# Eight places for the experts' weights in place of six, loops over groups of four experts, norm rows and bias in other buffers

## What is computed

```
def expert_block(args):
    xblk, e = args
    hcat = xblk @ w_up[e] + b_up[e]                 # 1024 -> 2048
    x_glu = jnp.minimum(hcat[:, 0::2], SWIGLU_LIMIT)
    x_lin = jnp.clip(hcat[:, 1::2], -SWIGLU_LIMIT, SWIGLU_LIMIT)
    act = x_glu * jax.nn.sigmoid(SWIGLU_ALPHA * x_glu) * (x_lin + 1.0)
    return act @ w_down[e] + b_down[e]              # 1024 -> 1024
...
contrib = y_slots[dest] * gate_sorted[:, None]
out = jax.ops.segment_sum(contrib, tok_sorted, num_segments=N)
...
h = layer_norm(DEEPNORM_ALPHA * h + ffn, ln2_g[l], ln2_b[l])
```

## Time and profile before

| | us |
|---|---|
| median of three timed runs (1586.87 to 1589.27) | 1588.96 |
| profiled execution | 1591.26 |
| its span, first to last instruction | 1589.5 |
| PE busy in the span | 1450.5 (91%) |
| weight loads of PE | 831.1 (52%) |
| DVE busy | 568.9 (36%) |
| ACT busy | 445.1 (28%) |
| experts' up products, L1239, 2048 of them | 452.6 |
| experts' down products, L1276, 1024 of them | 226.8 |

### The profile page before, as it was taken

One profiled execution on the slowest core, in us unless ns is written; L12 is line 12 of the kernel. 1 busy time (PEld: TensorE's weight loads), 2 busy tenths in 40 slices (PEclk: granted clock), 3 DMA queues, 4 the chain that ended last, 5 costly groups with the idle time before them and its releaser, 6 DMA issues. The chain is left out here.

```text
span 1589.5 us, 19014 instructions
## 1 busy us (share of the span) xinstructions
PE 1450.5 (91%) x7555; PEld 831.1 (52%) x7555; DVE 568.9 (36%) x1003; ACT 445.1 (28%) x569; POOL 36.7 (2%) x79
## 2 busy tenths in 40 slices
PE   7999999999999898898898898898896998789999
PEld 7988797333333333333333333333333877778887
DVE  3885456211120210210210211211114355557765
ACT  4654443221121111211112112112113135434443
POOL 1000030000000000000000000000000102000000
PEclk9999999999999999999999999999999998889999
DMA  8598997799999999999999999999997440335550
GB/s 246 164 310 264 329 335 249 322 426 429 428 428 428 428 429 429 429 429 428 428 428 428 428 428 428 428 429 428 429 429 250 133 159 28 105 107 186 186 185 27
DMA packets 130683, 516.92 MB, mean 325 GB/s; under 512 B 11173, under 2 KB 99086, under 8 KB 106030
## 3 DMA queue, kind: packets, MB, share of 16 engines
q1 hardware_dynamic: 130302, 515.11, 81.8%
q10 hardware_dynamic: 336, 1.18, 0.2%
HBM read 515.22 MB, written 1.05 MB: 325 GB/s over the span
## 5 line engine op out<-in xcount | busy, mean ns | idle before, releaser
L1239 PE MATMUL ps<-ring,xg 128*64 128x512 f32 x2048 | 452.6, 594 | 23.2 <-DMA ring<-in_expert_w_up 21.9
L1239 PEld LDWEIGHTS ps<-ring,xg 128*64 128x64 f32 x2048 | 143.9, 137 | 326.6 <-issue 269.4
L1352 DVE TENSOR_TENSOR glu<-ps,bupT 128x512 f32<-128x512 f32 x32 | 22.1, 692 | 739.3 <-PE ps L1248 739.3
L1276 PE MATMUL ps<-ring,act 128*64 128x512 f32 x1024 | 226.8, 595 | 6.9 <-DVE act L1362 6.9
L1276 PEld LDWEIGHTS ps<-ring,act 128*64 128x64 f32 x1024 | 70.7, 137 | 150.0 <-issue 127.9
L78 ACT ACTIVATE hrow<-ps 128x1024 f32<-128x1024 f32 x32 | 32.8, 1024 | 411.9 <-PE ps L1239 411.9
L1910 PE MATMUL ps<-h_halves,w_hi 128*128 128x512 f32 x352 | 125.8, 401 | 5.5 <-issue 5.5
L2007 DVE TENSOR_TENSOR w_lo<-ring,w_hi 128x2048 fp32r<-128x2048 f32 x37 | 84.8, 2292 | 70.7 <-ACT w_hi L78 70.7
L78 ACT ACTIVATE y<-ps 64x512 f32<-64x512 f32 x64 | 37.9, 592 | 241.0 <-PE ps L1276 240.7
L1912 PE MATMUL ps<-h_halves,w_lo 128*128 128x256 f32 x352 | 99.9, 284 | 0.0
L78 ACT ACTIVATE w_hi<-ring 128x2048 fp32r<-128x2048 f32 x37 | 70.6, 1909 | 69.1 <-PE ps L1912 41.7
(11 more groups left out here) (396 smaller groups left out, 1867.1 us busy)
## 6 DMA issues: line engine op xcount, KB each, us to landing
ring<-in_expert_w_up SPq DMA_DIRECT2D x128, 2048.0 KB, 23.4
ring<-in_expert_w_down SPq DMA_DIRECT2D x64, 2048.0 KB, 20.0
ring<-in_w_in SPq DMA_DIRECT2D x30, 1024.0 KB, 8.3
ring<-in_w_ada SPq DMA_DIRECT2D x24, 1024.0 KB, 6.0
ring<-in_w_gu SPq DMA_DIRECT2D x22, 1024.0 KB, 5.1
ring<-in_w_down SPq DMA_DIRECT2D x11, 1024.0 KB, 4.9
ring<-in_w_out SPq DMA_DIRECT2D x8, 1024.0 KB, 8.2
ring<-in_w_branch_sb SPq DMA_DIRECT2D x2, 1024.0 KB, 7.2
```

Source lines behind the costliest of these rows:

```text
L1239: last = nc.tensor.matmul(up[a2 * CAP:(a2 + 1) * CAP, u, :], k.xg[:, q, h * CAP:(h + 1) * CAP], w[:, c:c + 512], start=(q == 0), stop=(q = ...
L1276: last = nc.tensor.matmul(down[a2 * CAP:(a2 + 1) * CAP, :], k.act[:, m % 4, m // 4, :], w[:, c:c + 512], start=(m == 0), stop=(m == KF - 1 ...
L1352: link(nc.vector.tensor_tensor(k.glu[:, :, :, :], g, b[:, 0].to_broadcast(wide), ALU.add))
```

## The change

- `PLACES` is 8. Chunk i of a group goes to place i modulo 8; places 0 to 5 are those in the ring, 6 and 7 are a new buffer `more` of 32 KB a partition. There are eight semaphores `expert_in`, one a place.
- The loops of SP and PE go by groups of four experts (24 chunks, three turns through the eight places). PE's body holds two pairs in place of one; its loop has eight turns in place of sixteen. SP's loop has seven turns and a rest in place of 31. The loops of ACT and DVE stay loops over pairs.
- SP sends chunks 6 and 7, the first two of expert 1, at the head of `experts` without a wait on PE, behind the norm rows. After that chunk i waits until chunk i - 8 has been used (before: i - 6).
- The last uses of the ring's slots come at other counts, and the waits of the eight late loads follow (`2 * PLACES` for `PER`).
- To make room: `g2` and `b2` lie in the halves of `xT`; `b_dn` lies in the first 32 partitions of `hrow`; `k.bm` gets a buffer of its own, allotted after the experts' buffers are given back.
- Semaphores merged: `lb_ready` and `lf_ready` into one, `ln_in` of `branches` and `late_in` into one, with the counts of the waits adapted.

```diff
+PLACES = 8
+GROUP = 4 * CHUNKS
...
-def chunk_slot(c):
-    return (EARLY + 2 * c) % SLOTS
-def expert_chunk(k, c):
-    return k.ring[:, chunk_slot(c):chunk_slot(c) + 2, :].rearrange("p s n -> p (s n)")
-def load_expert(k, sp, a, e, c):
+def expert_chunk(k, i):
+    i %= PLACES
+    if i >= PLACES - 2:
+        return k.more[:, i - (PLACES - 2), :]
+    at = (EARLY + 2 * i) % SLOTS
+    return k.ring[:, at:at + 2, :].rearrange("p s n -> p (s n)")
+def expert_arrived(k, pe, group, i):
+    pe.wait_ge(k.expert_in[i % PLACES], group * (16 * GROUP // PLACES) + 16 * (i // PLACES + 1))
+    return expert_chunk(k, i)
+def load_expert(k, sp, a, first, i):
+    e, c = first + i // CHUNKS, i % CHUNKS
...
-    sp.dma_start(expert_chunk(k, c), src).then_inc(k.expert_in[c], 16)
+    sp.dma_start(expert_chunk(k, i), src).then_inc(k.expert_in[i % PLACES], 16)
...
             for dst, src in k.late_loads:
-                sp.dma_start(dst, src).then_inc(k.late_in, 16)
+                sp.dma_start(dst, src).then_inc(k.ln_in, 16)
             extra = extra_rounds(sp)
-            def refill(e, done):
-                for c in range(CHUNKS):
-                    sp.wait_ge(used, done + 2 * c + 2)
-                    load_expert(k, sp, a, e, c)
-            with sp.Fori(0, E - 1) as e:
-                refill(e + 1, e * PER)
+            for i in range(CHUNKS, PLACES):
+                load_expert(k, sp, a, 0, i)
+            def refill(first, done, lo, hi):
+                for i in range(lo, hi):
+                    sp.wait_ge(used, done + 2 * (i - PLACES + 1))
+                    load_expert(k, sp, a, first, i)
+            def rounds(done):
+                with sp.Fori(0, E // 4 - 1) as g:
+                    refill(g * 4, g * (2 * GROUP) + done, PLACES, GROUP + PLACES)
+                refill(E - 4, done + (E - 4) * PER, PLACES, GROUP)
+            rounds(0)
...
-                sp.wait_ge(used, done + (E * PER + q + 1 - PER))
+                sp.wait_ge(used, done + (E * PER + q + 1 - 2 * PLACES))
...
-            with pe.Fori(0, extra + 1) as r, pe.Fori(0, pairs) as p:
-                n = r * pairs + p
+            def pair(group, two, n):
                 pe.wait_ge(xg_ready, n + 1)
                 for h in range(2):
+                    first = (2 * two + h) * CHUNKS
...
                         if q % 2 == 0:
-                            pe.wait_ge(k.expert_in[q // 2], n * 32 + arrivals(q // 2, h))
-                        w = expert_chunk(k, q // 2)[:, (q % 2) * 2048:(q % 2 + 1) * 2048]
+                            chunk = expert_arrived(k, pe, group, first + q // 2)
+                        w = chunk[:, (q % 2) * 2048:(q % 2 + 1) * 2048]
...
+            with pe.Fori(0, extra + 1) as r, pe.Fori(0, pairs // 2) as g:
+                for two in range(2):
+                    pair(r * (pairs // 2) + g, two, r * pairs + g * 2 + two)
...
-            dve.wait_ge(k.late_in, 16 * len(k.late_loads))
+            dve.wait_ge(k.ln_in, 32 + 16 * len(k.late_loads))
...
-        k.gB, k.bm = k.x, k.xT[:, :, :].rearrange("p (t h) n -> p t h n", t=TT)
+        k.gB = k.x
...
-            k.g2, k.b2 = ht("g2", [P, D]), ht("b2", [P, D])
+            k.g2, k.b2 = (k.xT[:, 4 * n:4 * n + 4, :].rearrange("p k t -> p (k t)") for n in range(2))
...
-                k.gateT, k.b_dn = md("gateT", [E, T]), md("b_dn", [E, D])
+                k.gateT, k.b_dn = md("gateT", [E, T]), k.hrow[0:E, :]
+                k.more = md("more", [P, 2, 2 * SLOT])
...
+            k.bm = ht("bias_flipped", [P, TT, NA, T])
```

More of the change, by code:

```diff
@@ L613, in later @@
                     act.wait_ge(f_ready, 1)
-                    nc.scalar.activation(k.sgq[:, :, :], k.fbuf[:, :, :], ACT.Ln).then_inc(lf_ready, 1)
+                    nc.scalar.activation(k.sgq[:, :, :], k.fbuf[:, :, :], ACT.Ln).then_inc(lb_lf_ready, 1)
                 if i in (6, 7, 10, 11):
@@ L630, in _ @@
                     nc.scalar.activation(k.cact[:, :], k.cols[:, ROWS["c"]:ROWS["c"] + KD], ACT.Sigmoid)
-                    nc.scalar.activation(lb, k.lb[:, 8:12], ACT.Sigmoid).then_inc(lb_ready, 1)
+                    nc.scalar.activation(lb, k.lb[:, 8:12], ACT.Sigmoid).then_inc(lb_lf_ready, 1)
                 if i == 7:
@@ L740, in _ @@
                 if i == 2:
-                    dve.wait_ge(lb_ready, 1)
+                    dve.wait_ge(lb_lf_ready, 1)
                     nc.vector.tensor_tensor(k.cact[:, :], k.cact[:, :], k.cols[:, ROWS["c"]:ROWS["c"] + KD], ALU.mult)
@@ L753, in _ @@
                 if i == 5:
-                    dve.wait_ge(lf_ready, 1)
+                    dve.wait_ge(lb_lf_ready, 2)
                     dve.wait_ge(f_ready, 1)
@@ L829, in branches @@
         "logits_done", "top_negmax", "top_exp", "chosen", "pos_done"))
-    ln_in, gd, gb_done, ang_ready = (sem(n) for n in ("ln1_in", "gate_diag", "gate_rows", "angles"))
+    gd, gb_done, ang_ready = (sem(n) for n in ("gate_diag", "gate_rows", "angles"))
     gates, m, hT, xs = k.gates, k.xT, k.hT1, (k.xhi, k.xlo)
@@ L1034, in _ @@
             dve.wait_ge(k.x_in, 64)
-            dve.wait_ge(ln_in, 32)
+            dve.wait_ge(k.ln_in, 32)
             link(nc.vector.memset(k.mv[:, :, :], 0.0))
@@ L1155, in _ @@
             for dst, src in k.late_loads:
-                sp.dma_start(dst, src).then_inc(k.late_in, 16)
+                sp.dma_start(dst, src).then_inc(k.ln_in, 16)
             extra = extra_rounds(sp)
-            def refill(e, done):
-                for c in range(CHUNKS):
-                    sp.wait_ge(used, done + 2 * c + 2)
-                    load_expert(k, sp, a, e, c)
-            with sp.Fori(0, E - 1) as e:
-                refill(e + 1, e * PER)
+            for i in range(CHUNKS, PLACES):
[9 more added lines that the diff above has]
+            rounds(0)
             with sp.If(extra > 0):
                 with sp.Fori(0, extra) as r:
-                    refill(0, r * (E * PER) + (E - 1) * PER)
-                    with sp.Fori(0, E - 1) as e:
-                        refill(e + 1, r * (E * PER) + e * PER + E * PER)
+                    refill(0, r * (E * PER) + E * PER, 0, PLACES)
+                    rounds(r * (E * PER) + E * PER)
             done = extra * (E * PER)
@@ L1202, in scatter @@
                     last.then_inc(sc_done, 1)
-            def arrivals(c, h):
-                return 16 * (h + 1)
             for t in range(TT):
@@ L1267, in _ @@
                     for j in range(4):
-                        c4 = UP_CHUNKS + j // 2
                         if j % 2 == 0:
-                            pe.wait_ge(k.expert_in[c4], n * 32 + arrivals(c4, h))
-                        w = expert_chunk(k, c4)[:, (j % 2) * 2048:(j % 2 + 1) * 2048]
+                            chunk = expert_arrived(k, pe, group, first + UP_CHUNKS + j // 2)
+                        w = chunk[:, (j % 2) * 2048:(j % 2 + 1) * 2048]
                         for kk in range(2):
@@ L2134, in program @@
         k.last_used = k.sem("last_used")
-        k.expert_in = [k.sem(f"expert_in{i}") for i in range(CHUNKS)]
+        k.expert_in = [k.sem(f"expert_in{i}") for i in range(PLACES)]
         k.expert_used = k.sem("expert_used")
-        k.bcast_in, k.late_in, k.bias_in, k.bm_in = (k.sem(n) for n in (
-            "bcast_in", "late_in", "bias_in", "bm_in"))
+        k.bcast_in, k.ln_in, k.bias_in, k.bm_in = (k.sem(n) for n in (
+            "bcast_in", "ln_in", "bias_in", "bm_in"))
         k.evac, k.ln_var, k.ln_root, k.turned, k.hT_ready, k.sums, k.roots = (k.sem(n) for n in (
```

6 lines of the change are left out of this document (3 added, 3 removed).

## The result

| | before | after |
|---|---|---|
| median of the timed runs, us | 1589.12 | 1578.61 (1578.09 to 1580.43) |
| ratio, 95% interval | 1 | 0.9939 (0.9926 to 0.9951) |
| span of the profiled execution, us | 1589.47 | 1578.60 |
| start of the loop (first up product of PE) | 281.78 | 282.45 |
| last copy of y, which ends the loop | 1210.08 | 1202.09 |

The kernel is 0.61% faster, 10.5 us by the medians (1589.12 is the median of before with a fourth run, of three it was 1588.96) and 10.9 us by the two spans. Those 10.87 us split into three parts: the loop is 8.66 shorter, it starts 0.67 later, and the tail is 2.88 shorter.

What follows compares the result with a forecast made beforehand. The prediction took DMA transfers to bound the experts' loop from 540 us to its end. A term of -9.79 us, all others 0, gave span 1579.7, less 2.3 to the median: 1579.2 us, range 1575.0 to 1585.0.

Steps and rivals of the forecast that it cites:

- The bound: Experts' loop: DMA transfers bind from 540 us to its end and hold that end back by 31.2 us.
- The term of -9.79 us: Two early chunks fill the empty DMA stretch (hole) at 276 to 286 us, each saving 4.894 us: -9.79 us.
- The dent at 305 to 310 stays: Early loop: the dip to 370 GB/s, 0.3 MB or 0.7 us short, remains because releases only shift by two chunks.
- Deeper queue 0: Steady flow in the loop: up to two more chunks under way change the rate by nothing; between 0 and +2.1 us.
- The loops, norm rows, bias, late loads: 0: SP's and PE's longer loops, moved norm rows and down bias, and earlier late loads each cost 0 us.
- A start later than 276.8: Sign of being wrong: PE's first product with the down bias comes later than 276.8 us.
- PE's first wait near 760: In the loop, PE's first wait for a chunk moves from 540 to near 760 us, 9.8 / 2.66 = 3.7 pairs later.
- The end: Stage end: last up-chunk wait ends near 1181.3, y copied near 1200.3, hT releases the projection near 1221.6 us.
- The tail: After the last y: nothing there is touched by the change, so it moves forward as a block, no change in length.
- Rival 4: The dent at 305 also vanishes and half-clock stretches behind the stage fall kindly: gain 12 to 14 us, 1576; chance 0.06.
- Rival 2: PE's new loop slows it over 1.3 us a pair, losing part of the gain; chance 0.09 with other small losses.
- rival 3: PE's doubled loop body is fetched anew at each of seven returns, 38.5 us on PE: 1596.3 us, slower; chance 0.07.

Runs made afterwards that it cites:

- floor of 897.47: Kernel before with only an eighth of each expert's last down chunk loaded, PE's work unchanged: loop 897.47 us, median 1556.23 us, ratio 0.98.
- before, repeated: The kernel before run again unaltered for a second profile: loop 928.13 us, median 1587.53 us, ratio 0.9996.
- the two repeats of after: The changed kernel run twice more, unaltered: loops 919.63 and 919.26 us, medians 1577.87 and 1576.87 us, ratios 0.9936 and 0.9925 to the kernel before.
- third run of after: The changed kernel run once more, unaltered, the second of its repeats: loop 919.26 us, median 1576.87 us, ratio 0.9925 to the kernel before.
- version with six places: Changed kernel without the two more places and without early chunks, loops by four and moved buffers kept: loop 929.40 us, median 1587.33 us, ratio 1.0000.
- floor of after: Changed kernel with only an eighth of each expert's last down chunk loaded, PE's work unchanged: loop 897.97 us, median 1557.48 us, ratio 0.9801.

## Why the prediction was right, and where it was off

It said 1579.2 us in a range of 1575.0 to 1585.0; measured were 1578.61. The mechanism was right. That the time fits to 0.6 us is partly luck: the main term was 1.1 us too large, and a shorter tail, costed at nothing, made up for it. Step by step:

- **The bound.** Right. The transfers held the end of the loop back by 30.8 us (928.30 less the floor of 897.47; 31.2 predicted), and three changes of the byte stream alone (one chunk early, two early, rate down by 1.5%) move the end by 5.1, 8.0 and 13.7 us with PE's work unchanged.
- **The term of -9.79 us.** The mechanism was right, the size 1.1 us too large: the loop gained 8.7. The starts of the transfers show where the rest is. They are worked out from the start times of the stream's 16 KB packets, 128 to a chunk, chunks counted in the order in which they are sent; the row of a chunk is its ninth packet:

```
start, us                            before    after   difference   less the later start of the loop (0.67)
chunk 6                               286.8    275.3   -11.5
chunk 9                               302.3    293.3    -9.0
chunk 40                              455.1    446.3    -8.8        -9.5
chunk 180                            1140.3   1131.6    -8.7        -9.4
last wait of PE for an up chunk      1191.09  1183.11   -7.98       -8.65
last packet but 15                   1198.2   1189.6    -8.6
last packet                          1199.7   1191.8    -7.9
```

  In this pair the stream is ahead by 9.5 us from chunk 40 on, near the forecast of 9.8, and 0.7 us are lost between the start of a chunk's packets and its landing. Against before, repeated, the two repeats of after are ahead by 9.6 and 8.9 us at chunk 180, and by 8.5 and 8.9 at the last wait. So there are two losses.

  The first, 0.2 to 0.9 us, lies in the refills right behind the hole. In the third run of after it is 0.9 because the hole was too short there: PE started the loop only 7.7 us after the two early chunks were issued (10.6 in the first), the first refill was issued at 281.57 and chunk 8 began at 283.55, 2.0 us later where the first run has 1.1, for the two chunks were still under way.

  The second is a later landing. From a chunk's ninth packet to its landing a trace has one nearly steady time from chunk 30 on: 6.7 and 6.6 us in the two of before, 7.4 and 7.7 in the first two of after, but 6.5 in its third. The version with six places has 7.7, those with eight places and none or one filled early 6.8. So it is neither the deeper queue nor the new loops, since the same code has it in two runs and not in the third, and a queue of the old depth has it too. In the three traces that have it the last packet also starts 2.2 to 2.4 us after the last but 15, in the other five 1.3 to 1.8, as if the 16 DMA engines ran further apart; the packets carry no engine in the trace, so why some runs have it stays open.
- **The dent at 305 to 310 stays.** Right. With a full queue a chunk starts 4.9 us after the one before it. In before chunk 7 comes 0.9 us later than that, and chunks 10 and 11 together 0.8. In after chunk 9 comes 0.9 us late and chunks 12 and 13 together 1.1 (0.9 and 1.2 in the repeats). So the queue does see the releases of before shifted by two numbers, as was said, and the dent is at most half a microsecond deeper. The windows of fixed time make more of it (344 GB/s against 370, and 98 against 164 from 286 to 288), but they move against the loop with its start: the repeats of after show 370 and 393, and 377 and 401.
- **Deeper queue 0.** The rate is 428 against 429 GB/s and the pair takes 58.73 us in both. Right within 1 GB/s.
- **The loops, norm rows, bias, late loads: 0.** Right. Together they are worth nothing in time and +1.2 us in the loop (loops by four, six places), of which 1.1 are the later landing told above; PE's part is 0.5 (floor of after less floor of before), and hidden. The product with the down bias starts 0.67 us later than before, with no wait in its row, as all else there does. A start later than 276.8 was named as a sign of being wrong; here it is only the later start of the whole stage:

```profile
277.48 1.98 PE L1227 MATMUL ps<-hrow,gateT 32*128 32x512 f32 x4
```

- **PE's first wait near 760.** It came at 713.28. The working had 9.8 / 2.66 pairs; with the 8.7 us that were gained it is 3.3 pairs or 183 us, near 723, and waits fall only on the steps of an expert. A place predicted by dividing by a small difference carries the error of the term magnified: six places with the new loops, whose chunks land 1.0 us later than those of before, have this wait 54 us earlier than before.
- **The end.** Predicted 1181.3, 1200.3 and 1221.6, measured 1183.11, 1202.09 and 1223.36: all 1.8 later, of which 1.1 are the term's and 0.67 the later start.
- **The tail.** It was costed at no change, and gave 2.9 us. At half clock it spent 35.5 us in place of 51.2. The clock there varies in the same code as well: the repeat of before shows 41.3 us at half clock and a tail of 377.02, the third run of after 27.7 and 374.20, and the six places 34.1 and 373.97. That none of the 2.9 us is the change's is not shown. The tail covered the shortfall of the term, so the predicted time came out 0.6 us off where its main term was 1.1 us off. Rival 4 had this as a chance; by the loop alone that rival did not occur.

Rival 2 (PE takes over) and rival 3 (the body comes anew) fell by the floors of 897.47 and 897.97 and by the instruction queues. PE keeps 21.7 us of room in after (919.64 less 897.97, predicted 21.4).

## What to carry to other kernels

A stage that ends bound by bytes pays nearly in full for the bytes that its DMA engines did not move at its beginning (8.7 of 9.8 us here), hundreds of microseconds before the first engine waits; look for the stretch where the queue stood empty because every buffer was full, and size the new buffers by its missing bytes. Depth without early bytes bought 0.6 us here, and a finer cut of all transfers lost more by the rate (13.7 us) than the refills' timing could give (some 2 us). Compare versions by the length of the stage itself where start and clock of other stages move by more than the change.

## What the runs showed of the hardware

The rate of the stream still depends on the size of its transfers between 1 and 4 MB. For 128 partitions on one queue, with one core running:

| row | transfer | GB/s |
|---|---|---|
| 8 KB | 1 MB | 422 |
| 16 KB | 2 MB | 428 |
| 32 KB (up blocks; the down chunks 16 KB) | 4 MB (down 2 MB) | 431 |

Row and transfer changed together. The packets speak for the row: a row is one packet, and its median duration in the loop is 313 ns at 8 KB, 613 at 16 KB and 1216 at 32 KB, so twice the row takes 13 and 10 ns less than twice the time. That fits a fixed cost of some 10 ns a packet (an estimate; the expectation above had 9), but no run changed the one without the other. Over a stream of 900 us, the step from 16 to 8 KB cost 13.7 us, more than the whole change gained. The Trainium skill, DMA: Bandwidth & Descriptors, section Specifications, gives 435 GB/s as the fabric's ceiling and some 358 GB/s as the limit of the memory for one core; this case's 428 to 431 lie just below the first and well above the second, so that the second does not bind here, with one core alone.
